# A recurrent mixer rebuilt as one block: key projection first, the triangular substitution beside the other projections, chunks of 64 tokens in place of 32

## What is computed

```
xs  = h + (shifted h - h) * mu                       six mixtures, one for each of r, k, v, w, a, g
r, k, v = xs[:3] @ w_rkv                             three projections of 1024 x 1024
decay = exp(-exp(-0.5) * sigmoid(w0 + tanh(xw @ w_la) @ w_lb))
a   = sigmoid(a0 + (xa @ a_la) @ a_lb);   g = sigmoid(xg @ g_la) @ g_lb
kk  = k * k_k, normalised per head;       k = k * (1 + (a - 1) * k_a)
for each token t, for each of 16 heads of width 64, with a 64 x 64 state S:
    sa = S @ (-kk);  S = S * decay + sa (kk*a)^T + v k^T;  y = S @ r
y   = group norm of y per head, * ln_g + ln_b, + (sum r*k*r_k) * v, * g
out = x + y @ w_o
```

## Time and profile before

| what | us |
| --- | --- |
| three runs | 2202.36, 2205.94, 2195.92 (median 2202.36) |
| the profiled execution, its own time | 2182.94 |
| its span, from the first to the last instruction | 2181.2 |
| TensorE busy, and VectorE, ScalarE, GpSimd | 1899.2, 830.6, 508.2, 138.0 |
| mean granted TensorE clock, as a share of full speed | 0.926 |

### The profile page before, as it was taken

One profiled execution on the slowest core, in us unless ns is written; L12 is line 12 of the kernel. 1 busy time (PEld: TensorE's weight loads), 2 busy tenths in 40 slices (PEclk: granted clock), 3 DMA queues, 4 the chain that ended last, 5 costly groups with the idle time before them and its releaser, 6 DMA issues. The chain is left out here.

```text
span 2181.2 us, 28996 instructions
## 1 busy us (share of the span) xinstructions
PE 1899.2 (87%) x11494; PEld 1193.7 (55%) x11494; DVE 830.6 (38%) x1543; ACT 508.2 (23%) x807; POOL 138.0 (6%) x127
## 2 busy tenths in 40 slices
PE   6888599989989888898888789889988966898997
PEld 5675333333333333333333379779977656867996
DVE  7852511111111111111111266565543565446554
ACT  4421211101111110111111055345421141004442
POOL 3301210000000000000000000000000060200000
PEclk9968699999999999999999989999999986579998
DMA  7020699999999999999997275284425002108440
GB/s 271 34 107 1 257 404 428 428 428 429 428 428 429 428 429 428 429 428 429 428 428 323 101 295 188 78 308 155 154 74 204 0 20 66 52 1 308 154 154 30
DMA packets 99120, 554.34 MB, mean 254 GB/s; under 512 B 17473, under 2 KB 20418, under 8 KB 73618
## 3 DMA queue, kind: packets, MB, share of 16 engines
q1 hardware_dynamic: 99058, 553.49, 62.4%
HBM read 551.37 MB, written 2.10 MB: 254 GB/s over the span
## 5 line engine op out<-in xcount | busy, mean ns | idle before, releaser
L1009 PE MATMUL banks<-ring,xsT 128*64 128x512 f32 x2048 | 458.7, 598 | 41.9 <-DMA ring<-in_w_up 40.9
L1009 PEld LDWEIGHTS banks<-ring,xsT 128*64 128x64 f32 x2048 | 143.2, 137 | 351.3 <-issue 266.0
L1108 DVE TENSOR_SCALAR glu<-banks 128x512 f32<-128x512 f32 x32 | 22.1, 692 | 663.8 <-PE banks L1016 663.8
L1045 PE MATMUL banks<-ring,hT 128*64 128x512 f32 x1024 | 230.2, 603 | 22.0 <-ACT hT L1064 22.0
L1045 PEld LDWEIGHTS banks<-ring,hT 128*64 128x64 f32 x1024 | 71.5, 138 | 158.6 <-issue 130.5
L1546 PE MATMUL banks<-f_xT_hi,f_w_hi 128*128 128x256 f32 x512 | 146.8, 287 | 7.2 <-ACTq L1590 7.2
L1546 PE MATMUL banks<-f_xT_lo,f_w_hi 128*128 128x256 f32 x512 | 146.6, 286 | 0.0
L1546 PE MATMUL banks<-f_xT_hi,f_w_lo 128*128 128x256 f32 x512 | 146.6, 286 | 0.0
L1060 ACT ACTIVATE sig<-glu 128x512 f32<-128x512 f32 x32 | 20.1, 630 | 478.4 <-DVE glu L1108 478.4
L1546 PEld LDWEIGHTS banks<-f_xT_hi,f_w_hi 128*128 128x128 f32 x512 | 100.1, 195 | 9.4 <-DVE f_w_lo L1625 7.6
L1546 PEld LDWEIGHTS banks<-f_xT_lo,f_w_hi 128*128 128x128 f32 x512 | 100.1, 195 | 1.8
(11 more groups left out here) (383 smaller groups left out, 2992.6 us busy)
## 6 DMA issues: line engine op xcount, KB each, us to landing
ring<-in_w_up SPq DMA_DIRECT2D x128, 2048.0 KB, 24.7
ring<-in_w_down SPq DMA_DIRECT2D x64, 2048.0 KB, 20.3
ring<-in_ffn_w SPq DMA_DIRECT2D x32, 2048.0 KB, 7.8
ring<-in_sgu_in SPq DMA_DIRECT2D x8, 2048.0 KB, 7.6
m_raw<-in_w_in SPq DMA_DIRECT2D x7, 2048.0 KB, 10.3
ring<-in_w_rkv SPq DMA_DIRECT2D x6, 2048.0 KB, 20.4
ring<-in_sgu_out SPq DMA_DIRECT2D x4, 2048.0 KB, 7.6
ring<-in_w_out SPq DMA_DIRECT2D x1, 4096.0 KB, 16.4
```

The costliest lines, as they stand in the source:

```text
L1009: ins = nc.tensor.matmul(c.banks[CAP * h:CAP * (h + 1), bank, :], xsT[:, k, :], up_slot[k // 2][:, o:o + BANK], start=k == 0, stop=False)
L1045: ins = nc.tensor.matmul(c.banks[CAP * h:CAP * (h + 1), DOWN, :], hT[:, at:at + CAP], down_slot[half][:, o:o + BANK], start=k == 0, stop=k ...
L1108: v.tensor_scalar(glu[:, :], c.banks[:, GLU, :], LIMIT, None, ALU.min).then_inc(glu_ready, 1)
```

## The change

All of it lies in `rwkv_stage` and in the constant tensor of masks.

- CH becomes 64, so there are four chunks, two in each group of 128 tokens. The triangular systems stay 32 x 32 (SUB = 32): of each chunk the early and the late half are inverted on their own, 128 systems as before, and the coupling between the halves is added by matmuls (`own`, `cross`, `add_cross`) with one copy by VectorE between them.
- The three blocks become one, with no barrier inside and one arena of 22 units in place of the ring and the pool tile.
- The order of TensorE's work is: low-rank parts with the first bank of the key projection between them, the key projection, g, the sum of squares of kk, one bank of r, the spreading, a second bank of r, the gram AB, then the last two banks of r, the grams, the transposes, the bonus, the value projection, AKv, and then the steps that need the inverse.
- VectorE runs the substitution as soon as the AB triangles are back. It takes the last two banks of r and forms the bonus product in the course of it. AB is no longer masked, but copied by ScalarE and only its upper triangles are read. `right` holds the transposed a and AKv side by side, so that one matmul per head, chunk and half gives both P and u.
- The grams are 64 x 64 per chunk, masked by GpSimd in 16 multiplications of 128x384 in place of 32. GpSimd also forms a * (inverse decay).
- The scan starts from state 0 without multiplying it. GpSimd's addend follows the value projection. ScalarE squares the centred y.
- SyncE loads k first, then r, then v into k's place once the key projection is done; the rows ln_g, ln_b and w_o follow the value projection.

```diff
-CH = 32
+CH = 64
...
+                sp.wait_ge(k_done, 4)
+                for half in range(2):
+                    load_half(w_v, 2, half, v_in)
...
+                sp.wait_ge(ab_taken, 4)
+                for j in range(P // SUB):
+                    s, t = slice(SUB * j, SUB * (j + 1)), slice(SUB * (j % 2), SUB * (j % 2 + 1))
+                    sp.dma_start(dram_a[j].rearrange("n s t -> s n t"),
+                                 ab[s, :, :, t].rearrange("s c h t -> s (c h) t")).then_inc(a_out, 16)
+                sp.wait_ge(a_out, 16 * (P // SUB))
+                sp.dma_start(sys_a, dram_a.rearrange("j n s t -> (j n) s t")).then_inc(a_back, 16)
+                sp.wait_ge(solved, 1)
...
+                sp.wait_ge(v_done, 4)
...
+                for b in range(4):
+                    nc.gpsimd.tensor_tensor(two(bT, b), two(a, b), two(w_inv, b), ALU.mult).then_inc(aw_ready, 1)
...
+                for n in range(GRAMS):
+                    pool.wait_ge(gram_taken, n + 1)
+                    s = unit_heads(n)
+                    nc.gpsimd.tensor_tensor(s, s, mask[:, :, :].unsqueeze(2).to_broadcast([P, 3, 2, CH]),
+                                            ALU.mult).then_inc(gram_ready, 1)
...
+                pe.wait_ge(mixed, 3)
+                pe.wait_ge(k_in[0], 16)
+                to_features(w_k, MIX_K, BANKS_K[0], 0, k_done)
+                pe.wait_ge(hid_w, 1)
+                for b in range(4):
...
+                pe.wait_ge(mixed, 4)
+                pe.wait_ge(gate_in, 32)
+                low_rank(g_la, MIX_G, c.banks[:, 4, 0:T]).then_inc(g_la_done, 1)
...
+                for b in range(4):
+                    if b >= 2:
+                        pe.wait_ge(sig_taken, b - 1)
+                    second_rank(LORA, BANKS_A_LB[b], b)
+                pe.wait_ge(sig_taken, 3)
+                to_features(w_k, MIX_K, BANKS_K[1], 1, k_done)
+                pe.wait_ge(k_in[1], 16)
+                pe.wait_ge(sig_taken, 4)
...
+                pe.wait_ge(hid_g, 1)
+                to_features(w_k, MIX_K, BANKS_K[3], 3, k_done)
...
-                for m in range(3):
-                    pe.wait_ge(mixed, 4 + m)
-                    src, w = xs[(3 + m) % 2], w_rkv_sb[m]
-                    for b in range(4):
...
+                pe.wait_ge(kk_squared, 4)
+                matmuls(nc, c.banks[0:RH, BANK_SS, 0:T], [head_of[:, q, :] for q in range(KC)],
+                        [ar[:, q, 0, :] for q in range(KC)]).then_inc(ss_done, 1)
...
+                to_features(w_r, MIX_R, BANKS_R[0], 0, r_done)
+                pe.wait_ge(inv_ready, 1)
...
+                for b in range(4):
+                    for i in range(2):
+                        ins = nc.tensor.matmul(c.banks[:, BANKS_SPREAD[b], i * T:(i + 1) * T], head_to[:, 2 * b + i, :],
+                                               norms[:, 0, :], start=True, stop=True)
+                    ins.then_inc(spread_done, 1)
+                to_features(w_r, MIX_R, BANKS_R[1], 1, r_done)
+                pe.wait_ge(g_taken, 4)
+                for r in range(2):
+                    pe.wait_ge(chained, 2 * r + 2)
...
+                            for j in range(J):
+                                for par in range(2):
+                                    t, o = slice(tc * P + CH * j, tc * P + CH * (j + 1)), (tc * 4 + p % 4) * CH
+                                    ins = nc.tensor.matmul(c.banks[rows_of(j), BANKS_AB[2 * r + par], o:o + CH],
+                                                           bT[part(par), p, t], ar[part(par), p, 0, t], start=True,
+                                                           stop=True)
+                    ins.then_inc(ab_done, 1)
+                pe.wait_ge(r_in[1], 16)
+                to_features(w_r, MIX_R, BANKS_R[2], 2, r_done)
+                to_features(w_r, MIX_R, BANKS_R[3], 3, r_done)
...
+                        for j in range(J):
+                            t = slice(tc * P + CH * j, tc * P + CH * (j + 1))
+                            for par in range(2):
+                                nc.tensor.matmul(later(n + par)[rows_of(j), o:o + CH], bT[part(par), p, t],
+                                                 ar[part(par), p, 1, t], start=True, stop=True)
+                            for par in range(2):
+                                ins = nc.tensor.matmul(later(n + par)[rows_of(j), o + CH:o + 3 * CH],
+                                                       kT[part(par), p, t], ar[part(par), p, :, t], start=True,
+                                                       stop=True)
...
+                pe.wait_ge(mixed, 6)
+                for i in range(2 * TC):
...
+                    matmuls(nc, later(n + i), [xs[MIX_V][:, q, (i // 2) * P:(i // 2 + 1) * P] for q in range(KC)],
+                            [w_v[:, q, (i % 2) * BANK:(i % 2 + 1) * BANK] for q in range(KC)]).then_inc(v_done, 1)
...
+                pe.wait_ge(gram_ready, GRAMS)
...
+                pe.wait_ge(akv_taken, 4)
+                pe.wait_ge(x_back, 16 * (P // SUB))
...
+                            ins = nc.tensor.matmul(c.banks[rows_of(j), m % 4, i * P:(i + 1) * P],
+                                                   inv[rows_of(j), tc, 4 * hq + i, :], right[rows_of(j), tc, 4 * hq + i, :],
+                                                   start=i == 0, stop=False, skip_group_check=True)
...
+                            ins = nc.tensor.matmul(c.banks[late(j), 4 + m % 4, i * P:(i + 1) * P],
+                                                   ab[early(j), tc, h, SUB:CH], pu[early(j), :, tc, at_head(h)],
+                                                   start=True, stop=True)
...
+                            ins = nc.tensor.matmul(c.banks[late(j), m % 4, i * P:(i + 1) * P],
+                                                   inv[late(j), tc, 4 * hq + i, SUB:CH], crossed[late(j), m % 4, i, :],
+                                                   start=False, stop=True, skip_group_check=True)
...
+                for tc in range(TC):
+                    for m in range(4 * tc, 4 * tc + 4):
+                        own(m)
+                    for m in range(4 * tc, 4 * tc + 4):
+                        cross(m)
+                    for m in range(4 * tc, 4 * tc + 4):
+                        add_cross(m)
...
+                for b in range(4):
+                    pe.wait_ge(pu_taken, 4 + b + 1)
...
+                state_from_values(0)
+                state_from_sa(0)
+                pe.wait_ge(pt_taken, 4)
+                y_from_values(0)
+                y_from_values(1)
+                y_from_sa(0)
+                sa_from_state(1)
+                state_from_values(1)
+                state_from_sa(1)
+                y_from_sa(1).then_inc(y_inner, 1)
+                pe.wait_ge(y_inner, 1)
+                y_from_state(1).then_inc(y_done, 1)
+                y_from_values(2)
+                y_from_values(3)
+                sa_from_state(2)
+                state_from_values(2)
+                state_from_sa(2)
+                y_from_sa(2)
+                sa_from_state(3)
+                for ready in sa_ready:
+                    pe.wait_ge(ready, NCH - 1)
...
+                pe.wait_ge(y_inner, 2)
+                y_from_state(2)
...
+                for tc in range(TC):
+                    project(tc)
...
+                mix(MIX_K)
...
+                for b in range(4):
+                    dve.wait_ge(k_done, b + 1)
+                    for i in range(2):
+                        ins = vec.tensor_scalar(kk[:, 2 * b + i, :], c.banks[:, BANKS_K[b], i * T:(i + 1) * T],
+                                                c.col("k_k", 2 * b + i), None, ALU.mult)
...
+                    vec.scalar_tensor_tensor(two(kT, b), two(k_factor, b), 1.0, c.banks[:, BANKS_K[b], :], ALU.add,
+                                             ALU.mult).then_inc(k_read, 1)
...
+                    chain(dve, vec.tensor_tensor(two(kk, b), two(kk, b), c.banks[:, BANKS_SPREAD[b], :], ALU.mult))
+                    vec.tensor_tensor(two(bT, b), two(kk, b), two(bT, b), ALU.mult)
...
+                query(0)
+                query(1)
+                dve.wait_ge(a_back, 16)
+                dve.wait_ge(sys_ready, 2)
+                for t in range(1, SUB):
+                    w = work[:, 0:t * t].rearrange("p (j s) -> p j s", j=t)
+                    chain(dve, vec.tensor_tensor(w, sys_x[:, 0:t, 0:t],
+                                                 sys_a[:, 0:t, t].unsqueeze(1).to_broadcast([P, t, t]), ALU.mult))
+                    chain(dve, vec.tensor_reduce(sys_x[:, 0:t, t], w, AX.X, ALU.add))
+                    if t == 2:
+                        query(2)
+                    if t == 8:
+                        query(3)
+                        dve.wait_ge(q_ready, 4)
+                        vec.tensor_tensor(prod, ar[:, :, 1, :], kT, ALU.mult).then_inc(prod_ready, 1)
+                dve.nop().then_inc(solved, 1)
...
```

(16 more changed lines are left out.)

1013 lines of the change are left out of this document (502 added, 511 removed).

## The result

In the runs that stand beside the result the changed kernel takes 2105.23 us (median of 4, 2101.81 to 2106.35) against 2201.13 (median of 4, 2195.92 to 2205.94) before: ratio 0.9562 [0.9537, 0.9587], faster by 4.4%. In a later series of five rounds, on one chip, it is 2105.32 against 2184.43: 0.9634 [0.9606, 0.9661]. The new kernel's median is the same in both; the old one's differs by 17 us, so the change is worth 79 us in the later series and 96 in the first. The forecast, 2143 with a range of 2116 to 2173, had the direction right and lies 38 us too high.

What follows compares the result with a forecast made beforehand. In the mixer, projections, substitution (66 us with trips) and low-clock scan were taken as bounds; strands to 1794, inverse 28.5, scan to 1861.3 and tail to 1908.9 made the stage 59.4 shorter: 2143 us off the 2202.4 median, range 2116 to 2173.

Steps and rivals of the forecast that it cites:

- The sum up to AB: Mixer's start through the projections to the gram AB: K1 starts at 1666.0, AB takes 6 us and ends at 1717.6.
- Strand (a): From AB: ScalarE copy 0.8, trip 10.1, substitution 48.0 with r banks and bonus product inside, 7.8 back; inverse back at 1788.0.
- Strand (b): TensorE's work beside the substitution: R2, R3, grams 15, transposes, bonus, slow start 3.5, v 27.7, AKv 6.5; ends last, 1794.
- The inverse to P: Own, cross, add_cross, their copies and P's transposes between inverse and scan: 28.5 us, bounds 18 and 38, end 1822.5.
- The scan: 17 blocks of 32 records up to the last sa_from_state, at the low clock: 37.4 us plus 1.4 for VectorE's last take.
- the clock stays up in the quadrant matmuls: Rival, chance 0.17: full clock in the small matmuls; scan 14 less, inverse 5 less, strand (b) 6 less; 2118 us.
- The rule weighed: Skill page's rule that the clock opens under unbroken work; the forecast set it aside for the scan and took the low level.
- The tail: After the scan's last take: group norm of the first half 11.6, then 35.6, and 0.4 for the square; ends at 1908.9.
- The basis: Choice of starting time: 59 us off the profiled 2182.9 gives 2124; off the median 2202.4, which was forecast, 2143.
- the main gain: Substitution and its trips hidden beside TensorE's work; before, inverse back and AKv ready were at 1832.0, forecast at 1794.
- The addend did not slide into the scan: GpSimd's addend multiplications were put to end near 1810, before the scan; sliding into it would cost 7 us.
- the growth of the state: VectorE's four operations in the scan, 1.7 us, hidden behind the y blocks; without that cover, 1.7 twice.

Runs made afterwards that it cites:

- run with 32 rows: Changed kernel with 160 matmuls over 32 rows and 64 columns put in one piece ahead of the scan's second sa from the state; 2150.33 us.
- burst run: Old kernel with 16 wide matmuls (128 rows, 128 columns, 512 streamed) ahead of the scan's fifth step; 2198.55 us, 12.4 more than before.
- gap run: Changed kernel with the three blocks of sa from the state run nine times over, TensorE waiting four times in each for a ScalarE copy; 2206.02 us.

## Why the prediction was right or wrong

**The sum up to AB.** K1 was put at 1666.0 (measured 1666.9) and AB's end at 1717.6 (1718.0). Inside, two errors cancelled: AB took 2.09 us, not 6, and the spreading and R1 took 4.50 and 9.72 instead of 3.7 and 6.9. The spreading is 16 records over 16 rows, and the clock fell in it (0.83 in the us from 1704, then 0.50 up to 1711), with TensorE busy throughout. In the old kernel's trace the same 16 records end at full pace (3.72 us) and the clock falls right behind them (0.63 in the us from 1739). The run with 32 rows is like it; that the cause is the same is not shown.

**Strand (a).** Predicted back at 1788.0, measured 1788.07, with luck: two errors of 3.1 us cancelled. Substitution with its guests: 51.7 put, 48.6 taken; its first eight steps, before the masks started, were at 0.16 to 0.27 us a product. Trip back: 7.8 put, 10.9 taken, of which 4.7 lie between the issue of the write and that of the read; these were 2.7 in the old kernel's trace and 2.7 to 5.0 in the others of the changed kernel.

**Strand (b), the first step that failed.** "Sum: 1794." AKv was copied by 1780.3. The grams, "15 is taken", took 6.5; AKv 3.95 and not 6.5; and "3.5 taken" for a slow start of what follows was 0, the clock being 1.00 from 1718 to 1775. The strand of the substitution was last, as the 8.37 us of idle time ahead of 1788.07 show, and the path was 5.9 us shorter than forecast.

**The inverse to P.** 28.5 put, 29.0 taken (1788.07 to 1817.1). The 16 copies cost what they were priced at (11.3 us). The agreement of the rest is in part luck: I priced the matmuls between the two levels and the transposes at the low clock, and the clock, which had fallen in the idle time, was 1.00 from 1794 to 1813. The first group of 128 tokens took 14.1 us and the second 11.5, against 12.4 put; the transposes took 3.5 against 4 (the two groups and the transposes as I put them make 28.7, not 28.5).

**The scan, the second step that failed.** "Ten are like the 2.36 row and seven like the 1.97 row: 37.4", with 38.8 to the last take; measured 25.0 (1817.1 to 1842.1), so 13.8 less. The reason stands in "the trace disagrees for matmuls with 64 columns, so the sum takes the low level". I had carried the low clock of the old scan over to all narrow matmuls. The runs show that 64x64 matmuls hold a clock of 1.00 for 65 us, and leave, by elimination, the 32 rows as what lost it in the old scan. With chunks of 64 the products over the tokens of a chunk have 64 rows, and each of the scan's matmuls has. The rival "the clock stays up in the quadrant matmuls", with 2118 and a chance of 0.17, had this right, with 14 us for the scan and 6 for strand (b); only its 5 less for the inverse did not come (0.5 more). The rows that it named for itself, the old scan's first block at the full rate and the 64 rows of the new matmuls, deserved more weight. The rule weighed, the Trainium skill's "TensorE: Matmul & The Clock Gate", Part 1, that sustained work opens the clock, fits the new scan. The traces disagree with it in the burst run from 1905 on and in the 32-row run, each at 0.50 with TensorE busy without a break, in the 25 us of the gap run, and in the old scan, where TensorE is idle for only 1.1 of 56.8 us.

**The tail.** 47.6 put, 48.3 taken.

**The sum.** -5.9 (the strands), +0.5, -13.8 and +0.7 are -18.5, from 1908.9 to 1890.4.

**The basis, the third step that failed.** "59 off the profiled time is 2124; off the median, which I forecast, 2143." The 19 us between the two were not a part of the kernel: in the later series the old kernel takes 2183 to 2192 (medians or single runs), and the new one's profile (2105.73) lies at its median. So of the 38 us of error 18.5 are the two mis-sized steps and 19 the basis. A profile 0.9% under the median of three runs left both values open, and the range had to hold both bases.

**What was right.** The substitution is hidden beside r, grams and v: 44 us up to the return of the inverse, 31 of them by the run that undoes the cover of v and AKv. The prediction calls this the main gain; the traces give a larger one, 50 us, to the stretch from the scan's start to the tail, for which it had 36. How these 50 divide between half as many steps, the y blocks between them and the clock was not measured; only the clock has a price, for twelve blocks (30 against 17 us). The addend did not slide into the scan (its last multiplication ends at 1808.1), and the growth of the state stayed hidden.

**Open.** Which gaps lose the clock: lengths were not tried, and the traces have gaps of 0.64 to 0.88 us with and without a fall. What the 32-row matmuls of the inverse (cross and add_cross) do to the clock: they ran at 1.00 from 1794 to 1813, but right behind them there are 3 us at 0.50.

```profile
1814.00:1817.00 3.00, 3.00 (x15) 2.77 (x13) 0.00 (x0) 2.17 (x4) 0.00 (x0) 0.50 0.01 4
```

Twelve of the fourteen traces of the changed kernel and its edits have such a dip near the end of the first or the second group, two have none; the waits of 0.36 us between those matmuls are a rival cause, and nothing here divides the two. Whether GpSimd's masks lengthen the substitution as a whole was not measured. The 17 us between the old kernel's series were seen and not explained.

## What to carry to other kernels

Look at the rows of the array that a chain of small matmuls uses, and not only at its columns, and read the granted clock beside them: going from 32 to 64 tokens a chunk halved the number of steps and, at the same time, the clock stayed up, which was worth 14 us of the scan against a sum at the low rates; no count of instructions shows that. A wait of 0.7 us in the midst of small matmuls can cost many times its length (48 us for twelve in one run), where the small matmuls behind it don't bring the clock back; so look for such waits, and place them ahead of wide work where there is a choice. If an experiment delays one strand to see which decides, look for what the other strand takes from it: here both moved. And when the profiled time and the median disagree by more than what is to be told, run the old kernel again before choosing the basis, or let the range hold both.

## What was unexpected in the hardware

- The clock fell with TensorE busy without a break: in a piece of matmuls over 32 rows in one place (1.00 in the us from 1826, 0.50 from 1828, the piece having begun at 1824.21), and in the spreading over 16 rows. It held for 65 us with 64 rows, with 64 or 32 columns, and with 128x128 matmuls that stream only 64 columns (100 records in 11.38 us).
- Once low it stayed low through 64-row matmuls that had held it when high (1845.7 to 1870.8 in the gap run, 1855.9 to 1886.0 in the 32-row run). In the changed kernel's inverse block, whose 64x64 matmuls stream 128 columns and take turns over the array, it rose from 0.50 to 1.00 between 1793 and 1794 (they start at 1788.07), and between 1817 and 1818 it rose at the end of the 16 transposes that start at 1813.67.
- In the run with gaps it was lost behind one gap of 0.72 us in a stream of small matmuls that keep it without; gaps of 0.71, 0.78 and 0.88 us were outlasted elsewhere. The Trainium skill, "TensorE: Matmul & The Clock Gate", section "HAM oscillation — how this bites in real kernels", tells of short bursts of matmuls between waits for DMA of some 3 to 5 us, each of them throttled again; here a wait for ScalarE of 0.72 us was followed by a fall, so shorter waits than those of the page can matter.
- Matmuls of 64x64 that take turns over the four quadrants run side by side: AB's 128 records took 2.09 us, 0.016 us each, against 0.058 for the same form aimed at one place (16.43 us for 282).
- GpSimd's masks slow VectorE's products: the product of 4 numbers took 0.74 us beside the masks in the old kernel and 0.16 in the new one, where they had not begun; in the new one 81 numbers took 1.12 us beside them, 64 numbers 0.27 before.
